# Last FFN's gate and up products in Strassen-Winograd form: seven block products where there were eight, on one Trainium2 core

## The reference

```python
def swiglu_ffn(h, w_gate, w_up, w_down):
    return (jax.nn.silu(h @ w_gate) * (h @ w_up)) @ w_down
# layer 1: x = x + swiglu_ffn(rms_norm(x, g_ffn[1]), w_gate[1], w_up[1], w_down[1])
```

## Time and profile before

| | us |
|---|---|
| median of 3 runs | 2221.06 (2220.89 to 2221.09) |
| the profiled execution | 2222.57 |
| its span, first to last instruction | 2220.8 |
| TensorE matmul busy | 2198.6 (99%), 13856 matmuls |
| TensorE weight load busy | 1998.3 (90%) |
| VectorE busy | 1160.3 (52%) |
| ScalarE busy | 1058.6 (48%) |
| GpSimd busy | 1123.5 (51%) |
| the last FFN on half B, start of its first matmul to end of its last | 1806.1 to about 2212 |

### The profile page before, as it was taken

The page is one execution under the profiler, slowest core; times in us unless marked ns, Lnnn a source line. Parts: engine busy times, 40 slices in busy tenths (PEclk is TensorE's granted clock), DMA queues, the critical chain, the costliest instruction groups (busy, mean ns, idle before and its releaser), DMA issues.

```text
span 2220.8 us, 34667 instructions
## 1 busy us (share of the span) xinstructions
PE 2198.6 (99%) x13856; PEld 1998.3 (90%) x13856; DVE 1160.3 (52%) x1897; ACT 1058.6 (48%) x1720; POOL 1123.5 (51%) x568
## 2 busy tenths in 40 slices
PE   9899999999999999999999999999999999999999
PEld 7798878888889799999999898888888989999999
DVE  5998788953424555555553455555554152222223
ACT  6556664434435655555552465656565332222222
POOL 3786899975456434333334644433434543343443
PEclk9999999999999999999999999999999999999999
DMA  4111323333333522222222343222222223332222
GB/s 154 48 48 58 90 86 96 96 95 95 95 95 91 114 86 77 77 77 79 75 85 87 90 98 92 80 85 82 81 86 86 86 77 95 105 97 89 92 86 88
DMA packets 313646, 194.15 MB, mean 87 GB/s; under 512 B 40375, under 2 KB 286735, under 8 KB 313487
## 3 DMA queue, kind: packets, MB, share of 16 engines
q1 hardware_dynamic: 311608, 190.83, 28.9%
q10 hardware_dynamic: 1878, 1.11, 0.2%
HBM read 184.39 MB, written 5.10 MB: 85 GB/s over the span
## 4 chain that ended last, share of the span: by engine, by line
PE 92%; DVE 4%; POOL 2%; ACT 1%; issue 1%; DMA 0%; SPq 0%; DVEq 0%; POOLq 0%; ACTq 0%
PE ps L401 63%; PE ps L661 15%; PE ps L668 7%; PE ps L632 1%; PE ps L617 1%; PE ps L435 1%; DVE hB L1541 1%; DVE hBl L1546 1%; PE ps L593 1%; PE ps L592 1%; POOL accp L2119 1%; DVE ps L1649 1%; POOL rs L2098 0%; POOL wlo L2088 0%; PE ps L468 0%
## 5 line engine op out<-in xcount | busy, mean ns | idle before, releaser
L2088 POOL TENSOR_TENSOR wlo<-raw,whi 128x1024 fp32r<-128x1024 f32 x342 | 847.6, 2479 | 1031.6 <-PE ps L401 653.1
L958 ACT ACTIVATE whi<-raw 128x1024 fp32r<-128x1024 f32 x342 | 361.8, 1058 | 599.2 <-PE ps L401 341.6
L401 PE MATMUL ps<-hBh,whi 128*128 128x272 f32 x2112 | 435.2, 290 | 6.0 <-DVE gxA L1608 3.6
L401 PE MATMUL ps<-hBl,whi 128*128 128x272 f32 x2112 | 436.8, 290 | 0.8
L401 PE MATMUL ps<-hAh,whi 128*128 128x512 f32 x1056 | 410.5, 392 | 3.7 <-ACT s L1071 1.6
L401 PE MATMUL ps<-hAl,whi 128*128 128x512 f32 x1056 | 408.1, 390 | 0.2
L1744 DVE TENSOR_TENSOR x<-ps,x 128x512 f32<-128x512 f32 (+1 forms) x368 | 260.0, 707 | 249.2 <-PE ps L668 190.8
L401 PEld LDWEIGHTS ps<-hBh,whi 128*128 128x128 f32 x2112 | 331.8, 190 | 8.6 <-issue 4.1
L401 PEld LDWEIGHTS ps<-hBl,whi 128*128 128x128 f32 x2112 | 330.8, 189 | 2.4 <-DVE hBl L1546 2.4
L401 PE MATMUL ps<-hBh,wlo 128*128 128x272 f32 x2112 | 291.0, 290 | 0.0
L401 PEld LDWEIGHTS ps<-hBh,wlo 128*128 128x128 f32 x2112 | 273.5, 188 | 2.5 <-issue 1.9
(11 more groups left out here) (263 smaller groups left out, 3188.2 us busy)
## 6 DMA issues: line engine op xcount, KB each, us to landing
raw<-in_w_gate_dram SPq DMA_DIRECT2D x88, 512.0 KB, 3.8
raw<-in_w_up_dram SPq DMA_DIRECT2D x88, 512.0 KB, 3.8
raw<-in_w_down_dram SPq DMA_DIRECT2D x88, 512.0 KB, 3.6
raw<-in_w_pw_dram SPq DMA_DIRECT2D x38, 512.0 KB, 3.8
raw<-in_w_qkv_dram SPq DMA_DIRECT2D x32, 256.0 KB, 3.6
raw<-in_w_o_dram SPq DMA_DIRECT2D x64, 128.0 KB, 2.8
stage<-in_x_prompt_dram SPq DMA_DIRECT2D x8, 512.0 KB, 5.4
raw<-in_w_qkv_dram SPq DMA_DIRECT2D x8, 512.0 KB, 3.6
```

The lines of the kernel that those rows point to most:

```text
L401: ins = nc.tensor.matmul(o, wt[n % 2][:, P * k:P * (k + 1)], src[h][:, k, c0:c0 + w], start=start, stop=stop)
L958: nc.scalar.activation(whi[n % 2][:], raw[n % 2][:], ACT.Copy).then_inc(w_hi, 1)
L2088: nc.gpsimd.tensor_tensor(wlo[n % 2][:], raw[n % 2][:], f(whi[n % 2][:]), ALU.subtract).then_inc(w_lo, 1)
```

## The change

In the last FFN on half B, group 0 stays as it was. For groups 1 to 10 the gate part of a group (its two tiles, 1024 x 256 weights, times 1024 x 544 activations) is seen as a product of 2x2 blocks: weights by halves of the input features (kh) and by e, activations by kh and by chunk c of 272 tokens. The Winograd form of Strassen's scheme needs 7 products of blocks (`pair`, table WIN7) in place of 8; a product of blocks is 4 slices k x 3 = 12 matmuls of 272 columns, into one bank. The up part is done likewise. So 2 x 7 x 12 = 168 matmuls stand where there were 192.

What goes with it:
- **Activations**, once: VectorE writes four sums of blocks into `wtf`, each 128 x 4 x 272 elements, ScalarE their high parts `wth`, VectorE the low parts `wtl` (`low_t`). `x_norm` of this stage writes into `wtf` in place of `hB`.
- **Sums of weights**: four blocks S1 to S4 of 128x512 for each gate or up part, on GpSimd (`weight_sum`), 80 in all, into eight buffers `wsum`.
- **High and low parts** by blocks of 128x512, not by tiles of 1024: ScalarE the high part (`block_high`), VectorE the low part (`block_low`), which GpSimd made before. Blocks are counted by m; a group has 7 + 7 and four of w_down (two for each u), 18. Block m lies in the (m mod 4)th half of the two buffers of `whi` and `wlo`, so it takes the place of block m - 4.
- **Loads**: `raw` gets two more buffers (`wraw`), four in all; a buffer is reloaded when the low parts of what it held, sums included, are done (`room`).
- **Products put together**: 7 additions of 128x272 on VectorE for each part (`plus`) and one copy on ScalarE (`part_copy`), in buffers `sq`, `rs`, `wc`; silu and the multiplication then run out of SBUF.
- **PSUM**: the products take ring 1, one bank each; the down outputs take both rings in turn (`down_z`); the row transposes take ring 0.

The core of the diff:

```diff
+        WIN7 = [("A11", False, 0, 0), ("S2", True, 1, 1), ("A12", False, 1, 0), ("S3", True, 0, 1),
+                ("S1", True, 0, 0), ("A22", True, 1, 0), ("S4", False, 1, 1)]
...
+            def pair(w, G):
+                j = z_pair(G, w)
+                for e in range(2):
+                    load((w, 1, 2 * G + e))
+                for i, (_, by_t, kh, c) in enumerate(WIN7):
+                    key = ("P", w, G, i)
+                    z = z_first(j) + i
+                    take(key, "A", 1)
+                    if by_t and j == 0:
+                        pe.wait_ge(t_hi, 4)
+                        pe.wait_ge(t_lo, (1, 3, 4, 5).index(i) + 1)
+                    s, cols = z_slot(z)
+                    src = (wth, wtl) if by_t else (hi_["B"], lo_["B"])
+                    def product(wt, v, k, start=False, stop=False):
+                        return nc.tensor.matmul(bank(key), wt[s][:, cols.start + P * k:cols.start + P * (k + 1)],
+                                                src[v][:, 4 * kh + k, CWB * c:CWB * (c + 1)], start=start, stop=stop)
+                    pe.wait_ge(blk_hi, z + 1)
+                    for k in range(4):
+                        product(whi, 0, k, start=(k == 0))
+                        ins = product(whi, 1, k)
+                    ins.then_inc(blk_read, 1)
+                    pe.wait_ge(blk_lo, z + 1)
+                    for k in range(4):
+                        ins = product(wlo, 0, k, stop=(k == 3))
+                    ins.then_inc(pfull[place[key][0]], 1)
+                    if 1 <= G <= 4 and i == 2:
+                        y_group(2 * (G - 1) + j % 2, 0)
...
+            def down_z(G):
+                for u in range(2):
+                    load(("D", 1, G, u))
+                    z = 18 * G + (14 if G < NG - 1 else 0) + 2 * u
+                    s = z_slot(z)[0]
+                    pe.wait_ge(act_lo, 3 * FT + 2 * G + 2)
+                    for q in range(4):
+                        key = ("D", 1, "B", G, 4 * u + q)
+                        take(key, "B", q % 2)
...
+                def room(tag, i):
+                    if i < 4:
+                        sp.wait_ge(w_lo, n0 - 2 if i < 2 else n0)
+                        return
+                    g, r = divmod(i - 4, 6)
+                    sp.wait_ge(blk_lo, z_first(2 * g + r // 2) + 7 if r < 4 else 18 * g + 16 + 2 * (r - 4))
...
+            def block_high(m):
+                s = z_block(m)
+                t, cols = z_slot(m)
+                if m < 4:
+                    act.wait_ge(w_lo, first_z[0] - 1 + m // 2)
+                    act.wait_ge(whi_free, whi_read[first_z[0] - 2 + m // 2])
+                else:
+                    act.wait_ge(blk_lo, m - 3)
+                    act.wait_ge(blk_read, m - 3)
+                if s[0] == "D":
+                    landed_z(act, z_d_load(s))
+                elif BLOCK[s[2]][0] == "A":
+                    landed_z(act, z_load(s[1]) + int(BLOCK[s[2]][1]) - 1)
+                else:
+                    act.wait_ge(w_sum, 4 * s[1] + int(BLOCK[s[2]][1]))
+                nc.scalar.activation(whi[t][:, cols], w_block(s), ACT.Copy).then_inc(blk_hi, 1)
...
+                        for i, (kh, c) in enumerate(((0, 0), (0, 1), (1, 1), (1, 0))):
+                            act.wait_ge(t_sum, i + 1)
+                            z = (slice(0, P), slice(4 * kh, 4 * kh + 4), slice(CWB * c, CWB * (c + 1)))
+                            nc.scalar.activation(wth[z], wtf[z], ACT.Copy).then_inc(t_hi, 1)
+                hi()
+                act_high(1, "B", 0, 1, None)
+                for G in range(1, NG):
+                    j = 2 * (G - 1)
+                    for i in range(14):
+                        if i == 1:
+                            part_copy("G", G)
...
+                        if i == 7:
+                            act.wait_ge(c22_ready, j + 1)
+                            freed(act, ("P", "G", G, 5))
+                            act.wait_ge(act_lo, 3 * FT + 2 * G)
+                            nc.scalar.activation(s_[1][:], wc1[0][:], ACT.Silu).then_inc(w_silu, 1)
+                        if i == 8:
+                            for q in (2, 6):
+                                freed(act, ("P", "G", G, q))
+                            nc.scalar.activation(s_[0][:], wc0[0][:], ACT.Silu).then_inc(w_silu, 1)
+                    hi()
+                    for e in range(2):
+                        act.wait_ge(w_mul, 2 * G)
+                        nc.scalar.activation(ach[2 * (G % 2) + e][:], s_[e][:], ACT.Copy).then_inc(act_hi, 1)
+                    for _ in range(3):
+                        hi()
+                hi()
...
+            def block_low():
+                m = n_blk[0]
+                n_blk[0] += 1
+                t, cols = z_slot(m)
+                dve.wait_ge(blk_hi, m + 1)
+                if m < 4:
+                    full(dve, last_tile[first_z[0] - 2 + m // 2])
+                else:
+                    z_read(dve, m - 4)
+                nc.vector.tensor_tensor(wlo[t][:, cols], w_block(z_block(m)), f(whi[t][:, cols]), ALU.subtract
+                                        ).then_inc(blk_lo, 1)
...
+                for i, (out, p, q) in enumerate((((0, 0), (0, 1), (0, 0)), ((0, 1), (1, 1), (0, 1)),
+                                                 ((1, 1), (1, 1), (0, 0)), ((1, 0), (1, 0), (1, 1)))):
+                    if i:
+                        dve.wait_ge(t_sum, i)
+                    else:
+                        dve.wait_ge(h_ready["B"], h_need("ffn1", KD - 1))
+                    nc.vector.tensor_tensor(quarter(wtf, *out), quarter(wtf, *p), quarter(wtf, *q), ALU.subtract
+                                            ).then_inc(t_sum, 1)
+                def low_t(i):
+                    kh, c = ((0, 0), (0, 1), (1, 1), (1, 0))[i]
+                    dve.wait_ge(t_hi, i + 1)
+                    nc.vector.tensor_tensor(quarter(wtl, kh, c), quarter(wtf, kh, c), f(quarter(wth, kh, c)),
+                                            ALU.subtract).then_inc(t_lo, 1)
+                times_up(1, "B", 0, 0)
+                low_t(2)
+                low_t(1)
+                block_low()
+                low_t(0)
+                block_low()
+                low_t(3)
+                act_low(1, "B", 0, 0)
+                times_up(1, "B", 0, 1)
+                block_low()
+                act_low(1, "B", 0, 1)
+                for G in range(1, NG):
+                    for w in "GU":
+                        j = z_pair(G, w)
+                        key = [("P", w, G, i) for i in range(7)]
+                        c11, u2 = wc0[j % 2][:, 0:CWB], wc0[j % 2][:, CWB:]
+                        u3, c22 = wc1[j % 2][:, 0:CWB], wc1[j % 2][:, CWB:]
+                        def plus(out, i, term):
+                            full(dve, key[i])
+                            return nc.vector.tensor_tensor(out, bank(key[i]), term, ALU.add)
+                        block_low()
+                        freed(dve, key[0])
+                        block_low()
+                        plus(u2, 1, c11).then_inc(fr(key[1]), 1)
+                        block_low()
+                        freed(dve, key[1])
+                        plus(c11, 2, c11).then_inc(fr(key[2]), 1)
+                        block_low()
+                        plus(u3, 3, u2).then_inc(fr(key[3]), 1)
+                        block_low()
+                        if w == "U" and G <= 4:
+                            y_part(2 * (G - 1) + 1)
+                        freed(dve, key[3])
+                        plus(c22, 4, u3).then_inc(c22_ready, 1)
+                        plus(u2, 4, u2).then_inc(fr(key[4]), 1)
+                        block_low()
+                        dve.wait_ge(c22_ready, j + 1)
+                        plus(u3, 5, u3).then_inc(fr(key[5]), 1)
+                        block_low()
+                        freed(dve, key[4])
+                        plus(u2, 6, u2).then_inc(fr(key[6]), 1)
+                    block_low()
+                    for d in range(KD):
+                        if d == 1:
+                            dve.wait_ge(w_silu, 2 * G)
+                            freed(dve, key[5])
+                            nc.vector.tensor_tensor(s_[1][:], wc1[1][:], s_[1][:], ALU.mult).then_inc(w_mul, 1)
+                            for i in (2, 6):
+                                freed(dve, key[i])
+                            nc.vector.tensor_tensor(s_[0][:], wc0[1][:], s_[0][:], ALU.mult).then_inc(w_mul, 1)
+                        add_to_x(("D", 1, "B", G - 1, d))
+                        if d in (2, 3):
+                            act_low(1, "B", G, d - 2)
+                        if d in (4, 5):
+                            block_low()
+                    block_low()
+                block_low()
+                for d in range(KD):
+                    add_to_x(("D", 1, "B", NG - 1, d))
...
+                def weight_sum(j, i):
```

(20 more changed lines are left out.)

177 lines of the change are left out of this document (156 added, 21 removed).

## The result

The changed kernel takes 2197.35 us, the median of 4 runs (2195.79 to 2197.78); the kernel before, beside it, 2221.07 (2220.89 to 2222.13). The ratio is 0.9891, 95% interval 0.9874 to 0.9908, so 23.7 us are gone. Predicted were 2198.0 and a range of 2190 to 2210. The profiled execution took 2197.78 with a span of 2195.7.

A forecast was written before the change was run, and what follows sets the result against it. TensorE's instruction count was taken to bound the kernel. Terms -30.2 + 2.2 + 3.3 + 1.6 = -23.1 us from a profiled 2222.57 gave 2199.5, hence a median of 2198.0, range 2190 to 2210.

The forecast's parts named there:

- TensorE's saving: Last FFN, ten groups: each loses 24 matmuls of 0.1260 us on TensorE, 30.2 us in all.
- rival 4: Ten groups: TensorE pays 7 us for shorter runs into one bank, beside the stalls; 2205 us, chance 0.08.
- last sign: Ten groups: the first term is wrong if the matmul pitch is not 126 ns.
- The start: Group 1: TensorE stalls 2.3 us at block 2's low part and 1.0 at blocks 3 and 4; clock adds 1.6.
- The term of 1.6 for the clock: Behind group 1's gap: clock at 0.53 of full for 3.5 us, costing 1.6 us, added once.
- The groups: Down part's end: bank of addition d = 5 late by 0.1 to 0.4 us; 0.25 a group, 2.2 in nine.
- VectorE's load: Per late group: VectorE has 24.2 us of work in 33.2, so its sum does not bind.
- ScalarE's 15: Per late group: ScalarE's high parts and six or seven others take 15 us, so it does not bind.
- Turns: Late groups' down part: VectorE and GpSimd alternate on the shared port, one VectorE instruction after each of GpSimd's.
- Rival 1: Groups and start: no stall at all and the clock holds; -30.2 us, 2190.9 us, chance 0.17.
- Rival 2: Each group: VectorE sets the pace, adding 1.2 us a group; -13.3 us, 2207.8 us, chance 0.19.
- what would show it: Late group 33.2 to 33.6 us, VectorE busy 25 to 33; group 1 gap 2 to 4 us, clock near 0.5.

The follow-up runs named there:

- The version without waits, late up sums: The changed kernel with GpSimd's four sums of an up part held until the gate's fourth block has its low part; 2190.22 us.
- control: The changed kernel run again, unaltered, beside the kernel before; 2196.79 us, ratio 0.9889.
- short last product: The changed kernel with 9 of 12 matmuls left out of each part's seventh product, 180 in all; output not the reference's; 2177.14 us.
- addition first: The changed kernel with the two low parts in the down part placed behind additions d = 5 and 6; 2195.14 us.
- Narrow sums: The changed kernel with sums of weights covering 64 of 512 columns from group 2 on; output not the reference's; 2193.27 us.
- sums twice: The changed kernel with each sum of weights made a second time into the same block from group 2 on; 2204.84 us.
- start order: The changed kernel with VectorE's list at group 1's start reordered, low parts of blocks 2 and 3 ahead of the last low part of sums; 2192.96 us.
- the five with late sums: The changed kernel with up sums delayed: alone 2190.22, with earlier addition 2189.91, also reordered start 2191.21, shortened seventh product 2169.13, seventh product twice 2219.85 us.

## Why the prediction was right, point by point

**TensorE's saving, -30.2.** Right in kind, small by 0.8. The version without waits stands 31.0 under the kernel before. The twelve matmuls of a product on one bank run at 21.04 / 168 = 125.2 ns, where 48 on two banks ran at 126.0; 168 x 0.8 ns in ten groups are 1.3 us. With 192 in the list it is 24.05 / 192 = 125.3, so the shorter runs aren't dearer, and rival 4 is out. What makes them 0.7 to 0.8 ns cheaper no run here separates. By the prediction's own last sign ("wrong in the first term if the pitch is not 126 ns") the pitch was off by 0.6%. Beside it the estimate from the Trainium skill ("VectorE: DVE Perf Modes", the TRN2 errata) was 116 ns a matmul and 27.8 us; the measurement decides for 125.2 and 30.0, and for a saving that is a little larger than the page's.

**The start, 3.3 + 1.6.** The mechanism and its place were right. In the first profile the sizes were a wait of 1.9 and 3.8 x 0.45 = 1.7 us of clock; in the control's they were 1.4 and no clock behind the gap. The control is the fairer test of the gap, for its group 1 started at 1834.6, as predicted (1834.7): predicted 2.3, measured 1.4. The term of 1.6 for the clock was a guess from one stretch and didn't hold in each execution. Block 2's low part ended at 1839.3 in the first profile, at 1840.1 in the control, and not at 1841.0. In the hand count every instruction before it took a full turn of the port; VectorE's timeline, start of group 1, shows which did:

```profile
1833.53 2.38 DVE L2312 TENSOR_TENSOR wtl<-wtf,wth 128x1088 fp32r<-128x1088 f32 x1
1835.83 1.81 DVE L2015 TENSOR_TENSOR act0l<-s,act0h 128x544 fp32r<-128x544 f32 x1
1837.56 0.71 DVE L2010 TENSOR_TENSOR s<-ps,s 128x544 f32<-128x544 f32 x1
1838.19 1.12 DVE L2294 TENSOR_TENSOR wlo<-wraw,whi 128x512 fp32r<-128x512 f32 x1
1839.23 1.81 DVE L2015 TENSOR_TENSOR act1l<-s,act1h 128x544 fp32r<-128x544 f32 x1
```

The low part itself took 1.12 and not 1.8: part of the sum's hold had passed under the multiplication before it (L2010, whose first input comes from PSUM), as it does under the additions in the down part. And blocks 3 and 4, for which 1.0 was put, made no wait here. With the clock at 1.00 behind the gap there was a second wait for a low part, 0.3 us on PEld in the control and in short last product and 0.4 in addition first, so part of this is that TensorE at half clock came to them later; the 1.0 was too high either way.

**The groups, 2.2 in nine.** Right in the place (the bank of d = 5) and the kind, small in size. From the first matmul of group 1 to the last of the kernel's products the profiled execution takes 7.4 us longer than late up sums does; less 1.9 and 1.7 of the start, 3.8 is left for nine group changes, 0.4 each in place of 0.25. (The control by the same reckoning: 4.8 longer, less 1.4 and the second wait, leaves some 3.2.) Five late ones read 33.29, 33.15, 33.14, 33.31 and 33.50 against 33.05; groups 2 to 4, the change into group 2 and the last group hold the rest, up to 0.9 in one. Narrow sums, which take only this away, gave 3.5.

**The sum.** -31.0 + 3.8 + 1.9 + 1.7 = -23.6, measured -23.7; predicted -30.2 + 2.2 + 3.3 + 1.6 = -23.1. That the measured terms add up is no test, since the 3.8 is what was left over. The total was closer than its terms: the start was put too high by 1.3, the groups too low by 1.6, TensorE's saving too low by 0.8. That these nearly cancel, to 0.6 us, is luck.

**VectorE's load, 24.2 us.** Narrow sums read 25.2, which is that sum nearly without GpSimd: right within 1. ScalarE's 15 was 13.8.

**Port and rivals.** Turns, not a lock held by GpSimd: shown by the rows above and by sums twice. The Trainium skill ("SBUF — State Buffer", Who interferes with whom) calls the port an exclusive lock for a whole instruction; the trace agrees, with 1.81 beside a sum and 0.68 to 0.71 alone. Rival 1 (no stall, 2190.9) is what late up sums measure, 2190.2, for another order than the change's. Rival 2's 1.2 us a group takes twice the sums (1.4). Of what would show it, most came: a late group of 33.1 to 33.5 (33.2 to 33.6 given), VectorE at 28 of 33, low parts of 1.15 to 1.8 in the down part, and one gap on a low part in group 1. That gap was 1.9 us in the first profile and 1.4 in the control, under the 2 to 4 given, and the clock near 0.5 behind it came in the first and not in the second.

## What to carry to other kernels

Where one engine is busy all the time, its instruction count times its own pitch is the gain, and what is left to predict is whether the others stay ahead at each hand-over: write a timetable of one period with the port's turns in it, not a sum of busy times, and look for the first thing that is late. Work of an engine with much slack that takes a port from a busy one belongs where the busy one's list is loose; one condition that delayed four sums was worth 6.6 us between the medians, and left no wait on VectorE in the groups. Do the start of a stage by itself, since its lists are fuller than the steady state's. And take a second profile of the same kernel before a stretch of half clock is booked as a cost of the change.

## What was not expected of the hardware

**The clock behind the first tile of the last FFN.** At 1814.5 to 1818.0, where TensorE has waited for that tile's inputs, the profile before has a granted clock of 0.53, and it was taken for a fixed part of the kernel. It isn't. The same window reads 0.55 in the change run again, 0.58 in start order and 0.53 in short last product, but 1.00 in the first profile of the change and in the other eight kernels, though none of the edits lies ahead of it. It is worth up to 0.47 x 3.5 = 1.6 us, so single executions that lie within 1.5 us of each other tell nothing here without that row; group 1's start at 1833.3, predicted at 1834.7, is this. The profiled execution of the kernel before, 1.5 us above its median, may be another case. What decides it is open.

**Half clock after a short gap, in some executions.** In the first profile of the change TensorE stood idle for 1.9 us within 1836 to 1839.4, and the clock was at 0.55 over the next 3.8 us, in which TensorE was busy, and then at 1.00: there the gap cost nearly twice its length. In narrow sums and sums twice, with the same gap of 1.9, the clock fell too. In addition first, also 1.9, it did not, nor in the control and short last product, with 1.4. So a gap of this size can bring the half clock but need not. How often it did can be read only roughly from the mean granted clock of each execution, since 1.7 us of 2195 are 0.0008: of 25 executions with such a gap (the change twice and the four kernels just named) 21 have a mean of 0.998, of 31 of the six kernels without it (start order and the five with late sums) 27 have 0.999, and of 31 of the kernel before 29. The gap and the fallen clock go together over the executions, though the mean doesn't say in which stretch the clock was low.

**Steps are shorter than durations.** The next instruction of VectorE starts up to 0.1 us before the end of the last one in all these rows (1835.83 + 1.81 = 1837.64, next at 1837.56), so in steps a 512-wide low part costs 0.60 us and an addition of 272 columns 0.35, where their durations are 0.68 and 0.43.
